# Unread identity products in TensorE's waits while a mixture-of-experts layer routes its tokens

## The reference, cut to what matters

```python
h = x + merged @ w_out
xf = rms_norm(h, norm2)
pg = softmax(xf @ w_rg + b_rg)               # 4 groups, the best one is taken
le = (xf @ w_re + b_re).reshape(-1, 4, 8)    # 8 experts in a group, the best two are taken
for each of the 32 experts e:
    out += gate[:, e] * ((silu(xf @ w_eg[e]) * (xf @ w_eu[e])) @ w_ed[e])
y = h + out
```

## Time and profile before

| What | Value |
|---|---|
| Median of 3 runs | 1516.56 us (1513.1 to 1516.87) |
| The profiled execution | 1518.47 us |
| Its span in the trace | 1516.7 us |
| Mean granted TensorE clock | 0.945 of 2.4 GHz |
| TensorE products busy | 1344.7 us, 89% of the span, 5604 records |
| TensorE weight loads busy | 741.2 us, 5604 records |
| VectorE, ScalarE, GpSimd busy | 537.2, 341.9, 209.8 us |
| Moved by DMA | 210.32 MB |

### The profile page before, as it was taken

One profiled execution on the slowest core, in us unless ns is written; L12 is line 12 of the kernel. 1 busy time (PEld: TensorE's weight loads), 2 busy tenths in 40 slices (PEclk: granted clock), 3 DMA queues, 4 the chain that ended last, 5 costly groups with the idle time before them and its releaser, 6 DMA issues.

```text
span 1516.7 us, 15095 instructions
## 1 busy us (share of the span) xinstructions
PE 1344.7 (89%) x5604; PEld 741.2 (49%) x5604; DVE 537.2 (35%) x1483; ACT 341.9 (23%) x773; POOL 209.8 (14%) x289
## 2 busy tenths in 40 slices
PE   5999898999999995987599999999999999769781
PEld 5654446544444453555385544564444445445450
DVE  1278884100111235221245689730011113432114
ACT  2142465200001000211213325641000020112112
POOL 5011042000000001221150100600000000023213
PEclk9999999999999995999899999999999999979886
DMA  8302102502304116899671110033060050479975
GB/s 229 111 13 57 56 1 68 166 0 74 134 0 163 45 41 234 335 410 402 232 205 59 44 56 22 23 103 110 0 207 0 2 206 0 149 246 409 410 302 219
DMA packets 94795, 210.32 MB, mean 139 GB/s; under 512 B 25392, under 2 KB 34832, under 8 KB 94720
## 3 DMA queue, kind: packets, MB, share of 16 engines
q1 hardware_dynamic: 81792, 183.90, 34.3%
q0 software_dynamic: 12928, 25.43, 4.8%
HBM read 196.29 MB, written 27.78 MB: 148 GB/s over the span
## 4 chain that ended last, share of the span: by engine, by line
PE 79%; DMA 7%; issue 4%; DVE 3%; ACT 3%; SPq 2%; PEldq 1%; PEld 0%; POOL 0%; POOLq 0%; ACTq 0%; DVEq 0%
PE bank L696 33%; PE bank L967 9%; PE bank L1001 9%; PE bank L1041 7%; PE bank L727 3%; PE bank L1052 3%; PE bank L865 2%; PE bank L1034 2%; PE bank L879 2%; DMA more<-in_w_eu 1%; DMA ring<-in_w_eu 1%; PE bank L776 1%; DMA uv<-xd,mb 1%; PE bank L682 1%; PE bank L892 1%
## 5 line engine op out<-in xcount | busy, mean ns | idle before, releaser
L696 PE MATMUL bank<-ring,xt 128*128 128x512 f32 (+1 forms) x1120 | 433.8, 544 | 2.7 <-issue 1.8
L696 PEld LDWEIGHTS bank<-ring,xt 128*128 128x128 f32 x1120 | 214.0, 193 | 204.3 <-issue 190.4
L1626 DVE TENSOR_TENSOR scr<-scr,bank 128x512 f32<-128x512 f32 x20 | 13.8, 689 | 368.6 <-PE bank L967 368.6
L1001 PE MATMUL bank<-ring,xt 128*128 128x512 f32 x320 | 141.0, 594 | 0.0
L512 POOL TENSOR_SCALAR stat<-stat 128x1 f32<-128x1 f32 (+1 forms) x27 | 11.4, 424 | 802.0 <-ACT uv L1121 622.7
L1265 ACT ACTIVATE scr<-bank,stat 128x512 f32<-128x512 f32 x40 | 25.3, 684 | 347.9 <-PE bank L696 347.8
L1001 PEld LDWEIGHTS bank<-ring,xt 128*128 128x128 f32 x320 | 59.4, 190 | 67.9 <-issue 67.9
L1041 PE MATMUL bank<-ring,xt 128*64 128x256 f32 x480 | 75.4, 416 | 18.8 <-issue 18.8
L727 PE MATMUL bank<-ring,xt 128*128 128x512 f32 x160 | 76.6, 613 | 0.0
L1041 PE MATMUL bank<-qkv,xt 128*64 128x256 f32 x256 | 67.2, 422 | 9.4 <-issue 9.4
L967 PE MATMUL bank<-ring,att 128*128 128x512 f32 x160 | 72.5, 596 | 2.2 <-ACT sgt L1257 1.8
(11 more groups left out here) (264 smaller groups left out, 1774.6 us busy)
## 6 DMA issues: line engine op xcount, KB each, us to landing
ring<-in_w_in SPq DMA_DIRECT2D x12, 2048.0 KB, 9.2
ring<-in_w_ed SPq DMA_DIRECT2D x36, 512.0 KB
ring<-in_w_eg SPq DMA_DIRECT2D x30, 512.0 KB
ring<-in_w_eu SPq DMA_DIRECT2D x30, 512.0 KB
qkv<-in_w_eg SPq DMA_DIRECT2D x16, 512.0 KB
qkv<-in_w_eu SPq DMA_DIRECT2D x16, 512.0 KB
ring<-in_w_out SPq DMA_DIRECT2D x4, 2048.0 KB, 12.8
more<-in_w_ed SPq DMA_DIRECT2D x16, 512.0 KB
```

Source lines behind the costliest of these rows:

```text
L696: mm = pe.matmul(out, xt[:, k, t * P:(t + 1) * P], rhs[:, k, :], start=(k == 0), stop=(k == KD - 1))
L1001: mm = pe.matmul(banks[5 + n % 3][:, :], xt[:, k, t * P:(t + 1) * P], w[:, k, :], start=(k == 0), stop=(k == KD - 1))
```

## The change

A helper `idle(n)` issues n products of the 128x128 identity with itself into PSUM bank 3, which nobody reads. Eight groups of it are put into each layer: before the last tile's transposes and before and behind its route, behind the counts, behind L1019, behind the table, and between the first two `rows_step`. They wait for nothing and signal nothing; 76 products are added in each layer, and nothing is removed or moved.

```diff
+            def idle(n):
+                for _ in range(n):
+                    pe.matmul(banks[3][:, 0:P], idm, idm, start=True, stop=True)
...
+                idle(3)
                 norm_transposes(1, (NT - 1,), L)
+                idle(3)
                 route(NT - 1)
+                idle(12)
...
                 pe.matmul(banks[5][:, 0:flat], ones, scr[:, P + flat:P + 2 * flat], start=False, stop=True).then_inc(count_psum, 1)
+                idle(6)
                 pe.wait_ge(need_ready, prior("need_ready", L) + 1)
                 pe.matmul(banks[6][:, P:P + EXPERTS + 1], need_rows, before[0:EXPERTS, 0:EXPERTS + 1],
                           start=True, stop=True).then_inc(start_psum, 1)
+                idle(18)
...
                 mm.then_inc(table_psum, 1)
+                idle(28)
                 pe.wait_ge(table_ready, prior("table_ready", L) + 1)
...
                 rows_step(0)
+                idle(6)
                 rows_step(1)
                 up_step(0)
```

## The result

The changed kernel takes 1507.61 us in the median of ten runs (1502.68 to 1512.11), the kernel before 1515.07 (1513.08 to 1517.75). The ratio is 0.9947, with a 95% interval of 0.993 to 0.9963: 8.0 us less, between 5.6 and 10.6. The forecast was 4.7 us less.

A forecast was written before the change was run, and what follows sets the result against it. The routing chain up to the first up step, partly at half clock, was taken as the bound, since the weight stream waits for it. 0.8 + 1.85 + 2.06 = 4.7 us off 1516.56 gave 1511.8, range 1507.5 to 1516.5.

The forecast's parts named there:

- The Trainium skill's rule on transposes: Transposes don't count as activity for full clock as products do; as a rival 1517.9 us, chance 0.08.
- The wait for the gather: Behind the table: wait grows to 9.4 and 9 us, 28 products fill 6.2, some 3 us idle mostly lose the clock.
- The rise: Clock returns 3.4 us after first transposes begin; rows steps through first up step take 8.5 us, gaining 1.85 and 2.06.
- no fall: Rival: 28 products run longer or the clock bears 3 us of idleness; 7.8 us won, 1508.8 us, chance 0.17.
- the gathers: Gather's start, after an earlier table: 0.8 us gained in layer 0, 0 in layer 1.
- the steps: Rows steps through first up step with the clock high all along: 6.95 us, a gain of 3.4 and 3.6.
- The case that I had thought likeliest: The forecast: clock falls in the gather's wait in both layers, still 4.7 us won, 1511.8 us, chance 0.60.

The follow-up runs named there:

- seam: The changed kernel with 50 more products behind layer 0's last expert block, in the wait between the layers; 1509.19 us, ratio 0.9966 to the kernel before.
- gather_group_22: The changed kernel with 22 products in place of 28 in the wait for the gather; 1509.14 us, ratio 0.9964 to the kernel before.
- no_gather_group: The changed kernel without the 28 products behind the table; 1511.18 us, ratio 0.998 to the kernel before.
- rows_first: The changed kernel with the rows' transfers ahead of the loads of experts 6 and 7 on SyncE's queue; 1502.82 us, on a second chip 1503.49.

## Why the prediction was wrong in size

**What held.** The mechanism, step by step: the short groups fit their waits and hold the clock; the route takes 1.98 us (1.8 forecast); the gather is released by the landing rows and not by the table; the first up step takes 3.6; and what it ends earlier is won in full. The Trainium skill's rule on transposes ("TensorE: Matmul & The Clock Gate", "Part 4: PE-mode transpose") would have cost the whole gain. Rows 4 and 9 speak against it; the changed kernel's profiles have no rise in the rows steps, so they add nothing.

**The step that failed** is "The wait for the gather": some 3 us of idleness would stay behind the 28 products, and "3 us will mostly lose the clock". Some 2 us stayed, and the clock was not lost. Two sizes were off, both in one direction.

- The wait was taken as 9.4 and 9 us. It is 8.3 (586.84 to 595.17) and 8.6 (1320.80 to 1329.40). The table is 3.1 us earlier in layer 0 and not 3.5 (16.2 us after the projection against 592.24 - 572.97 = 19.3), 1.6 in layer 1 and not 2. The gather in layer 0 is not 0.8 but 1.4 us earlier (24.4 us after the projection against 25.8 for its landing): its release gave 0.9, and its transfer took 4.24 us against 4.72, where I had feared a longer one.
- The 28 products were taken as 6.2 us, 0.22 each. They take 6.52, 0.23 each.
- So 1.88 and 2.15 us stay, not 3. At this length the clock held, four times out of four in the two profiles of the change. What the prediction said of 3 us itself came out: behind the same products the clock fell with 2.65 and 2.87 us in seam and in 3.59 us in gather_group_22, and held through 3.40 once. Before, it had fallen with 2.17 once and 2.22, so length alone doesn't decide, and that it held each time with some 2 us left may be luck in part.

A size in "The rise" was off as well, though it didn't come into play in the change: where the clock did fall in that wait, it rose 4.6 to 5.7 us after the first rows step began and not 3.4 (no_gather_group, gather_group_22). From there to the end of the up step it took 9.1 to 9.7 us and not 8.5.

With that, the rival "no fall" became the course of events. Its price was near: 7.8 us forecast, 7.6 in the segments, 8.0 by the ratio. That is partly luck: the gathers gave 0.7 us more than forecast and the steps 1.0 less. By terms, layer 0: gather 1.4 (0.8 forecast), rows steps and up step 7.45 us against 10.35, 2.9 (3.4 forecast; the six products and the tails leave 2.69 us between the rows steps in place of 2.45). Layer 1: 7.42 against 10.56, 3.1 (3.6 forecast), and 0.1 from the gather (0 forecast). The case that I had thought likeliest, a fall in both layers, was priced too high: no_gather_group, where both came, is 3.0 us below the kernel before (2.8 in the segments), beside 4.7 forecast. (gather_group_22 came to 5.5, but with a fall in only one layer of its profile.) The odds, 0.60 to 0.17, were wrong because a difference of two long numbers (9.4 less 6.2) carried all of it: errors of 0.4 to 1.1 us in the one and 0.3 in the other took away a quarter to two fifths of what was to be left.

**Open.** The change scatters over 9 us (1502.68 to 1512.11) where rows_first scatters over 5 in its two runs together. With all 28 products, late rows with a fall behind them were seen in one profile, that of seam, but gather_group_36, which leaves little room for such falls, scattered over 7. The rest wasn't traced.

## What to carry to other kernels

Where an engine's clock falls in waits, cover the waits with real products that end just before the wait does; size each group by what the clock will be when it starts, because a group that starts at half clock stands in front of the work it was meant to speed up. The worth of it is what runs at half clock behind the wait and is followed by everything else, here two rows steps and one up step a layer, and not the short steps inside the chain. When one input of a wait gets earlier, look at the other one next: here the rows' transfer behind 3 MB of weights, which cost nothing to move (1.0001 alone) and gave 2 to 3 us more.

## What the runs showed that I had not expected

- Products of 8 columns, with TensorE and its weight loads busy throughout, left the clock at 0.50 for some 45 us in a row in layer 0 and 37 in layer 1; the same number of 128 columns kept it at 1.00.
- A 20 KB transfer landed 12.3 to 14.2 us after its issue behind two experts' loads, and 1.9 to 3.3 us after it ahead of them.
- The clock fell behind 2.65 us of idleness in one profile and held through 3.40 us in another.
